# One decoder layer on one core: the second residual's rows kept on chip, and two regions moved into the expert weights' ring

## The chip, the cores and the metric

The kernel runs on one core of one Trainium2 chip. The metric is device time in microseconds (us) of one execution. Three runs of the kernel before gave 961.46, 961.75 and 962.04 us, median 961.75.

## What is computed

One decoder layer on 512 tokens of width 1024, all in float32. Token mixing (dilated attention, a convolution module, an mLSTM) is computed first; its branches are gated, merged, projected and added to x. The second part, in which the change lies, is, cut to what matters:

```
x2  = x + merged @ w_out                     # the second residual, (512, 1024)
h   = rmsnorm(x2, g_ffn)
# hierarchical MoE: top-1 of 4 groups, then top-2 of its 8 experts; 32 experts in all
hb  = silu(xb @ w_gate[e]) * (xb @ w_up[e])  # (1024, 256) each
y   = (hb @ w_down[e]) * weight              # (256, 1024)
x3  = x2 + y of the token's two experts
x4  = x3 + sigmoid(rmsnorm(x3, g_ple) @ w_pg) * (p @ w_pp)
out = rmsnorm(x4, g_final)
```

All 32 experts are run whatever the routing: each on one block of up to 64 of its tokens, and a few further blocks only if an expert has more tokens.

## The kernel before, in words

Engines run programs of their own and meet at semaphores. SyncE (SP in the profile) issues all loads and stores except the indirect ones, in an order written out by hand; a wait in its program holds back everything behind it. GpSimd (POOL) issues the indirect transfers: for each expert one gather of token rows (`normed` to `mT`, line 2210) and one scatter of result rows (`mT` to `expert_rows`, line 2216).

**Weights.** An expert's weights are an "up" piece (gate and up, 2 MiB, `up_weights`, line 551, or in halves, line 556) and a "down" piece (1 MiB, `down_weights`, line 559). They go round a ring of `RING = 7` slots; `up_w` and `down_w` say where each slot lies. Most slots are regions of the 128 KiB (per partition) tensor `arena`, one is in `yT`, the up slot of expert 6 is `hT`. The down slots of index 5 and 6 are the two halves of `x_sb`, the tensor that holds x2. In addition `early_down` names two regions of `arena`, at 120 and at 80 KiB, that are used once, for the down pieces of experts 7 and 8 (`down_of`, with a semaphore of their own, `early_loaded`). So before the first expert runs, the up pieces of experts 0 to 6 and the down pieces of experts 0 to 8 are loaded or under way.

**Why x2 leaves the chip.** Since its place is given to weights, each 128-token row block of x2 is stored to `x2_rows` in memory (`store_x2`, lines 582 to 584; 512 KB each, four of them) beside the store of its normalised rows (`store_n2`, line 588). SP then waits for these stores and for all readers of the block before it loads down pieces 5 and 6 into `x_sb`. After the experts 26 and 27 are through, `x2_row_back` (line 623) loads block 0 and 1 back, then the weights of the last stage follow (`w_pg`, `w_pp`, `p`), and behind the second half of `w_pg` blocks 2 and 3 are loaded back and `g_final`.

**The expert loop.** For n from 7 on, SP issues the up piece of expert n+1 when `up_done` says that the up products of expert n-6 are through (line 551 behind its wait), and the down piece of expert n when `down_done` says that those of expert n-7 are. For n = 7 and 8 there is no down piece in the loop. TensorE runs up(n) when both pieces of expert n have landed, then turns the next gathered block (line 1439), then runs down(n-1). All matrix products go through the helper at line 1076, the small transpose between up and down is line 1457. ScalarE applies the sigmoid (line 975), copies (line 980) and scales the result rows (line 987); VectorE multiplies (lines 2075, 2082, 2084).

**The tail.** With the last expert through, TensorE computes `p @ w_pp` (32 products of tile `hT`), ScalarE rounds `w_pg` (line 995), VectorE takes its remainder (line 2105) and copies (line 2111). When the last scatter has landed, SP loads `expert_rows` back (line 652), and VectorE adds the two result rows to x2 (lines 2134 and 2135) in its program behind six remainders. TensorE turns the sum (line 1356) and multiplies it by `w_pg`.

Of the kernel before, what the change touches and what calls it, by code (L numbers as in the profile page):

```python
# [28 lines left out]
F32 = mybir.dt.float32  # L29
# [6 lines left out]
P = 128  # L36
D = 1024
SEQ = 512
T = SEQ // P
# [25 lines left out]
RING = 7  # L65
# [58 lines left out]
def build(nc, x, consts, chan, g_mix, r_bias, g_final, w_cm, w_tm, w_if, w_gate, w_branch, w_out,  # L124
          w_router, w_expert, w_pg, w_pp, pT, out):
    normed = nc.dram_tensor("normed", [SEQ, D], F32, kind="Internal").ap()
    expert_rows = nc.dram_tensor("expert_rows", [2 * SEQ, D], F32, kind="Internal").ap()
    x2_rows = nc.dram_tensor("x2_rows", [SEQ, D], F32, kind="Internal").ap()
    bound_rows = nc.dram_tensor("bound_rows", [4 * SEQ], F32, kind="Internal").ap()

    with ExitStack() as ctx:
        offset_of = {}

        def sb(name, shape, dt=F32):
            offset_of[name] = -(-nc.sbuf_base // 32) * 32
            return ctx.enter_context(nc.sbuf_tensor(name, shape, dt))

        def sem(name):
            return ctx.enter_context(nc.semaphore(name))


        x_sb = sb("x_sb", [P, T, D])
# [29 lines left out]
        class Place:  # L172
# [63 lines left out]

        yflat = yT[:, :, :, :].rearrange("p b r s -> p (b r s)")
        ple_rows = [Place(at, memory).take(D) for at, memory in ((16, yflat), (20, yflat), (16, arena), (20, arena))]
        x_flat = x_sb[:, :, :].rearrange("p t d -> p (t d)")
        hT_flat = hT[:, :, :].rearrange("p k s -> p (k s)")  # L240
        up_w = [Place(16).take(4096), yflat[:, 0:4096]] + [Place(at).take(4096) for at in (48, 88, 0, 64)] + [hT_flat]
        down_w = [Place(32).take(2048), yflat[:, 4096:6144]] + [Place(at).take(2048) for at in (40, 112, 104)]\
            + [x_flat[:, 0:2 * D], x_flat[:, 2 * D:4 * D]]
        early_down = [Place(120).take(2048), Place(80).take(2048)]
        EARLY = RING + len(early_down)

        def down_of(n):

            return early_down[n - RING] if RING <= n < EARLY else down_w[n % RING]

        pg_w = [Place(0).take(4096), Place(24).take(4096)]
        pg_low = [parts_in("pg_low0", "arena", [P, 4096])[:, :], parts_in("pg_low1", "arena", [P, 4096], 24 * 256)[:, :]]
# [106 lines left out]
        gates_step = sem("gates_step")  # L359
        picked = sem("picked")  # L360
        routing_mm = sem("routing_mm")
        x2_spilled = sem("x2_spilled")
        prefix_ready = sem("prefix_ready")
        columns_read = sem("columns_read")
        bound_moved = sem("bound_moved")
# [59 lines left out]
        x2_ready = sem("x2_ready")  # L425
        x2_squared = sem("x2_squared")
        n2_ready = sem("n2_ready")
        n2_stored = sem("n2_stored")
        x2_turned = sem("x2_turned")
# [8 lines left out]
        ple_mm = sem("ple_mm")  # L438
        ple_copied = [sem("ple_first_half_copied"), sem("ple_second_half_copied")]
        we_loaded = [sem(f"we_loaded{b}") for b in range(RING)]  # L440
        early_loaded = sem("early_loaded")
        idx_copied = sem("idx_copied")
        rows_gathered = [sem(f"rows_gathered{b}") for b in range(ROWS)]
        rows_turned = sem("rows_turned")
# [7 lines left out]
        down_done = sem("down_done")  # L452
        y_scaled = sem("y_scaled")
# [4 lines left out]
        rows_loaded = [sem(f"rows_loaded{t}") for t in range(T)]  # L458
# [34 lines left out]
        def _(sp):  # L493
# [56 lines left out]
            def up_weights(n):  # L550
                sp.dma_start(up_w[n % RING], w_expert[n, :, 0:4096]).then_inc(we_loaded[n % RING], 16)  # L551

            def up_weights_in_halves(n):
                for half in range(2):
                    part = slice(half * 2048, (half + 1) * 2048)
                    sp.dma_start(up_w[n % RING][:, part], w_expert[n, :, part]).then_inc(we_loaded[n % RING], 16)

            def down_weights(n):
                sp.dma_start(down_of(n), w_expert[n, :, 4096:6144]).then_inc(early_loaded if RING <= n < EARLY else we_loaded[n % RING], 16)

            sp.wait_ge(yconv_ready, ROUNDS)
            sp.dma_start(wo, w_out).then_inc(wo_loaded, 16)
# [5 lines left out]
            for t in range(T):  # L568
                if t == T - 1:
                    sp.wait_ge(branch_done, 3 * KD - 1)  # L570
                sp.dma_start(x_sb[:, t, :], x[t * P:(t + 1) * P, :]).then_inc(x_loaded[t], 16)
            down_weights(RING)
            sp.wait_ge(merged, FREE + KD)
            for n in range(2):
                up_weights(n)
# [3 lines left out]
            up_weights(2)  # L579
            up_weights(3)  # L580

            def store_x2(t):
                sp.wait_ge(x2_ready, T + t + 1)
                sp.dma_start(x2_rows[t * P:(t + 1) * P, :], x_sb[:, t, :]).then_inc(x2_spilled, 16)

            def store_n2(t):
                sp.wait_ge(n2_ready, t + 1)
                sp.dma_start(normed[t * P:(t + 1) * P, :], n2[t % 2]).then_inc(n2_stored, 16)

            for t in range(T - 1):  # L590
                store_x2(t)
                store_n2(t)
            sp.wait_ge(x2_spilled, (T - 1) * 16)
            sp.wait_ge(x2_squared, T + 2)
            sp.wait_ge(x2_turned, T + 2)
            down_weights(5)
            sp.wait_ge(x2_mm, 2 * T)
            down_weights(3)
            store_x2(T - 1)
            down_weights(4)  # L600
            store_n2(T - 1)
            up_weights_in_halves(4)
            up_weights_in_halves(5)
            sp.wait_ge(logits_done, T)
            up_weights_in_halves(6)
            sp.wait_ge(x2_spilled, T * 16)
            sp.wait_ge(x2_turned, 2 * T)
            down_weights(6)
            sp.wait_ge(x2_squared, 2 * T)
            sp.wait_ge(n2_stored, T * 16)  # L610
            down_weights(RING + 1)
            for n in range(RING, NEXP):
                if n == RING:
                    sp.wait_ge(up_done, 1)
                    up_weights(n)
                if n + 1 < NEXP:
                    sp.wait_ge(up_done, n + 2 - RING)
                    up_weights(n + 1)
                if n >= EARLY:
                    sp.wait_ge(down_done, n + 1 - RING)  # L620
                    down_weights(n)
            def x2_row_back(t):
                sp.dma_start(x_sb[:, t, :], x2_rows[t * P:(t + 1) * P, :]).then_inc(rows_loaded[t], 16)

            sp.wait_ge(up_done, 26)
            sp.wait_ge(down_done, 27)
            for t in range(2):
                x2_row_back(t)
            sp.dma_start(pg_w[0], w_pg[0, :, :]).then_inc(pg_loaded[0], 16)
            sp.wait_ge(up_done, 28)  # L630
            sp.dma_start(pple_w, w_pp).then_inc(pw_loaded, 16)
            sp.dma_start(p_in, pT).then_inc(pw_loaded, 16)
            sp.wait_ge(down_done, 29)
            sp.dma_start(pg_w[1], w_pg[1, :, :]).then_inc(pg_loaded[1], 16)
            for t in range(2, T):
                x2_row_back(t)
            sp.dma_start(gfin_sb, g_final.partition_broadcast(P)).then_inc(params_loaded, 16)
            sp.wait_ge(routed, 1)
            n_over = sp.value_load(ctl[0:1, 0:1], min_val=0, max_val=MAX_OVER)
# [434 lines left out]
        def _(pe):  # L1074
            def mm(out, lhsT, rhs, start=True, stop=True):
                return pe.matmul(out, lhsT, rhs, start=start, stop=stop)  # L1076
# [377 lines left out]
            def turn_hidden(n, b2):  # L1454

                pe.wait_ge(h_swished, n + 1)
                pe.transpose(HT[:, 0:P], hs[b2], ident).then_inc(h_turned, 1)  # L1457

            def down(n, b2, w, y_free):

                pe.wait_ge(hx_ready, n + 1)
                y_free()
                for j in range(2):
                    for side in range(2):
                        at = j * 1024 + side * 512
                        last = mm(Y[b2][side * BLK:(side + 1) * BLK, :], hx[b2][:, j, :], w[:, at:at + 512], j == 0, j == 1)
                last.then_inc(down_done, 1)
# [3 lines left out]

            turn_block(0, 0, rows_gathered[0], 16, first=True)
            def expert_down(n):
                if n == RING:
                    pe.wait_ge(early_loaded, 32)
                down(n, n % 2, down_of(n), nothing if n < 2 else lambda: pe.wait_ge(y_scaled, n - 1))

            for n in range(NEXP):
                pe.wait_ge(we_loaded[n % RING], (n // RING + 1) * 32 + (16 if n % RING in (4, 5, 6) else 0) - (16 if n >= RING and n % RING < 2 else 0))
                up(n, n % 2, up_w[n % RING], nothing if n < 2 else lambda: pe.wait_ge(h_swished, n - 1),  # L1480
                   between=(lambda: turn_hidden(n - 1, (n - 1) % 2)) if n else None)
                if n + 1 < NEXP:
                    slot = (n + 1) % ROWS
                    turn_block(n + 1, slot, rows_gathered[slot], ((n + 1) // ROWS + 1) * 16)
                if n == 3:
                    over_table()
                if n:
                    expert_down(n - 1)
                if n == OVER_KNOWN:
                    pe.wait_ge(routed, 1)  # L1490
                    n_over = pe.value_load(ctl[0:1, 0:1], min_val=0, max_val=MAX_OVER)
# [27 lines left out]
            for t in range(T):  # L1519
# [3 lines left out]
                for half in range(2):  # L1523
                    n = 2 * t + half
# [28 lines left out]
        def _(dve):  # L1553
            steps = [0]

            def chain(ins):

                steps[0] += 1
                ins.then_inc(dve_step, 1)
                dve.wait_ge(dve_step, steps[0])  # L1560
# [569 lines left out]
                                      h_high[part].bitcast(F32), ALU.subtract).then_inc(h3_split, 1)  # L2130

            for t in range(T):
                dve.wait_ge(rows_loaded[t], 48)
                chain(dve.tensor_tensor(x_sb[:, t, :], x_sb[:, t, :], yk[t][:, 0, :], ALU.add))  # L2134
                dve.tensor_tensor(x_sb[:, t, :], x_sb[:, t, :], yk[t][:, 1, :], ALU.add).then_inc(x3_ready, 1)  # L2135
                if t == 0:
                    ple_second_half(3)
                    h3_remainder(0)
                    for k in range(6, KD):
                        pg_remainder(k)  # L2140
                if t == 1:
                    h3_remainder(1)
# [183 lines left out]
```

## Time and profile before

| | before |
|---|---|
| median of three runs | 961.75 us |
| the profiled execution, its device time | 961.88 us |
| its span, first to last instruction | 960.1 us |
| TensorE busy / VectorE / ScalarE / GpSimd | 93% / 51% / 36% / 20% |
| bytes moved by DMA | 182.44 MB |
| mean granted TensorE clock | 0.977 of full |
| chain that ended last: TensorE / DMA / VectorE | 80% / 11% / 4% |

The device time is 1.8 us above the span, and 0.13 us above the median of the runs. The profile is of one execution. A share of DMA is the mean busy share of the core's 16 DMA engines; where it stands at 1.01 to 1.03 all of them are busy all the time. Megabytes here are 10^6 bytes: a down piece of 1024 KB is 1.049 MB, an up piece 2.097 MB, a row block of 512 KB 0.524 MB.

### The profile page before, as it was taken

How to read it: one execution, taken by the hardware profiler on the slowest of the kernel's cores; microseconds unless marked ns; L12 is line 12 of the kernel's file. 1: busy time of each engine (PE TensorE's matmuls, PEld its weight loads, DVE VectorE, ACT ScalarE, POOL GpSimd, SP SyncE). 2: the span in 40 equal slices, each digit the busy share in tenths (PEclk: the TensorE clock that was granted, in tenths of full speed). 3: DMA queues.
4: the chain of work that ended last, by engine and by line, in shares of the span. 5: the costliest groups of instructions: out<-in, count | busy, mean ns of one | idle time of the engine just before them, and what ended most of it. 6: DMA issues, size and time to landing. Idle time of an engine off the chain costs nothing.

```text
span 960.1 us, 12099 instructions
## 1 busy us (share of the span) xinstructions
PE 893.9 (93%) x4762; PEld 655.0 (68%) x4762; DVE 492.7 (51%) x999; ACT 342.3 (36%) x574; POOL 194.2 (20%) x169
## 2 busy tenths in 40 slices
PE   5999999999999989999999999947999988779986
PEld 4788788778878858788888888844555534334675
DVE  6378679669767978633333444463111111112755
ACT  5534453544435366422222332111111111113464
POOL 0052263335226332000000000011323322221000
PEclk9999999999999999999999999968999999999998
DMA  7520321212030110822222038889999999998401
GB/s 271 176 92 19 132 67 44 98 61 84 1 132 23 66 34 1 355 116 99 95 81 86 36 131 350 308 330 363 385 417 420 421 420 421 421 418 357 183 23 66
DMA packets 29088, 182.44 MB, mean 190 GB/s; under 512 B 5840, under 2 KB 6352, under 8 KB 18152
## 3 DMA queue, kind: packets, MB, share of 16 engines
q1 hardware_dynamic: 23912, 173.26, 46.0%
q0 software_dynamic: 5120, 8.41, 2.4%
q8 instruction: 38, 0.62, 0.3%
q14 instruction: 18, 0.15, 0.0%
HBM read 175.33 MB, written 14.69 MB: 198 GB/s over the span
## 4 chain that ended last, share of the span: by engine, by line
PE 80%; DMA 11%; DVE 4%; ACT 2%; issue 1%; SPq 1%; DVEq 0%; POOLq 0%; ACTq 0%
PE bank L1076 76%; DMA arena<-in_w_expert 9%; PE bank L1439 1%; PE bank L1166 1%; DMA mT<-normed,table 1%; DMA x_sb<-in_x 1%; DMA expert_rows<-mT,table 1%; PE bank L1457 1%; DMA arena<-expert_rows 0%; SPq L551 0%; PE bank L1367 0%; DVE x_sb L2135 0%; PE bank L1092 0%; DVE x_sb L2134 0%; ACT arena L679 0%
## 5 line engine op out<-in xcount | busy, mean ns | idle before, releaser
L1076 PE MATMUL bank<-mT_parts,low_parts 128*128 128x512 f32 (+1 forms) x456 | 178.5, 394 | 0.0
L1076 PE MATMUL bank<-arena,cst 128*64 128x256 f32 (+2 forms) x904 | 132.7, 433 | 15.6 <-DMA arena<-in_w_expert 10.7
L1076 PE MATMUL bank<-mT_parts,x_parts 128*128 128x512 f32 (+1 forms) x328 | 132.4, 404 | 0.0
L1076 PE MATMUL bank<-hT_parts,x_parts 128*128 128x512 f32 (+1 forms) x328 | 129.1, 394 | 0.0
L2075 DVE TENSOR_TENSOR cst<-bank,chn 128x512 f32<-128x512 f32 x32 | 22.1, 692 | 184.3 <-PE bank L1439 184.3
L1620 DVE TENSOR_TENSOR low_parts<-arena,x_parts 128x1024 fp32r<-128x1024 f32 (+1 forms) x44 | 62.8, 1427 | 98.4 <-ACT x_parts L691 98.1
L1076 PEld LDWEIGHTS bank<-arena,cst 128*64 128x64 f32 (+1 forms) x904 | 63.1, 140 | 71.7 <-issue 29.0
L1076 PEld LDWEIGHTS bank<-mT_parts,low_parts 128*128 128x128 f32 (+1 forms) x456 | 85.0, 186 | 21.2
L1672 DVE SCALAR_TENSOR_TENSOR arena<-arena,chn 128x512 f32<-128x512 f32 x116 | 99.2, 912 | 0.0
L2210 POOL DMA_INDIRECT mT<-normed,table x32 | 33.0, 1031 | 282.1 <-DVE table L2023 268.5
L1076 PE MATMUL bank<-arena 128*128 128x64 f32 (+9 forms) x400 | 79.9, 332 | 1.2 <-DVE small L1769 1.2
L2195 POOL TENSOR_TENSOR arena<-arena 128x128 f32<-128x128 f32 (+3 forms) x32 | 40.3, 1260 | 176.1 <-ACT arena L787 176.1
L1076 PEld LDWEIGHTS bank<-mT_parts,x_parts 128*128 128x128 f32 (+1 forms) x328 | 61.1, 186 | 15.9 <-DVE low_parts L1620 0.9
L1076 PEld LDWEIGHTS bank<-hT_parts,x_parts 128*128 128x128 f32 (+1 forms) x328 | 61.0, 186 | 15.1 <-issue 0.7
L1076 PEld LDWEIGHTS bank<-arena 128*128 128x128 f32 (+1 forms) x400 | 56.3, 189 | 21.5 <-issue 14.3
L2216 POOL DMA_INDIRECT expert_rows<-mT,table x32 | 32.4, 1014 | 162.1 <-ACT mT L987 155.6
L787 ACT ACTIVATE arena<-arena,small 128x384 f32<-128x384 f32 (+3 forms) x32 | 32.6, 1020 | 55.5 <-DVE small L1769 55.5
L1076 PE MATMUL bank<-mT_parts,cm_high_b 128*128 128x512 f32 x128 | 51.3, 409 | 0.0
L928 ACT ACTIVATE arena<-bank 128x512 f32<-128x512 f32 x24 | 14.2, 595 | 102.2 <-PE bank L1076 102.2
L1076 PE MATMUL bank<-hT_parts,cm_high_b 128*128 128x512 f32 x128 | 49.2, 393 | 0.0
L987 ACT ACTIVATE mT<-bank,table_weight 128x512 f32<-128x512 f32 x32 | 22.0, 687 | 69.8 <-PE bank L1076 69.8
L1076 PE MATMUL bank<-x_parts,mT_parts 128*128 128x384 f32 x128 | 44.6, 349 | 0.0
(288 smaller groups left out, 1560.0 us busy)
## 6 DMA issues: line engine op xcount, KB each, us to landing
arena<-in_w_expert SPq DMA_DIRECT2D x21, 2048.0 KB
arena<-in_w_expert SPq DMA_DIRECT2D x24, 1024.0 KB, 13.7
arena<-in_w_cm SPq DMA_DIRECT2D x32, 512.0 KB, 3.6
arena<-in_w_gate SPq DMA_DIRECT2D x8, 1536.0 KB, 6.7
yT<-in_w_expert SPq DMA_DIRECT2D x5, 2048.0 KB
x_sb<-in_w_expert SPq DMA_DIRECT2D x8, 1024.0 KB
arena<-in_w_tm SPq DMA_DIRECT2D x4, 1536.0 KB, 7.7
arena<-in_w_branch SPq DMA_DIRECT2D x8, 768.0 KB, 8.2
```

The source lines that it names most:

```text
L787: act.activation(sc[:, u % 2, 0:n], sc[:, u % 2, 0:n], ACT.Exp, bias=nmx[:, u % 2:u % 2 + 1], accum_out=den[:, u:u + 1]).then_inc(exps_don ...
L928: act.activation(sgm[:, br], (PA, PB, S_16)[br][:, :], ACT.Sigmoid).then_inc(gate_read, 1)
L987: act.activation(yr[slot], Y[b2][:, :], ACT.Copy, scale=table_w(n)).then_inc(y_scaled, 1)
L1076: return pe.matmul(out, lhsT, rhs, start=start, stop=stop)
L1166: last = pe.transpose(TR[:, j * P:(j + 1) * P], psm[:, u % 2, j * P:(j + 1) * P], ident)
L1439: last = pe.transpose(TR[:, k * P:(k + 1) * P], xr[slot][:, k * P:(k + 1) * P], ident)
L1620: dve.tensor_tensor(low, weights, high.bitcast(F32), ALU.subtract).then_inc(done, 1)
L1672: dve.scalar_tensor_tensor(cacc[:, j % 2], ypad[:, j:j + SEQ], weight, cacc[:, j % 2], ALU.mult, ALU.add).then_inc(conv_step, 1)
L2075: dve.tensor_tensor(xT[b2], TR[:, :].rearrange("p (k h s) -> p k h s", k=KD // 2, h=2), chn[:, G_FFN:G_FFN + KD].rearrange("p (h k) -> p k ...
L2195: pool.tensor_tensor(dst[:, 0:n], sc[:, u % 2, 0:n], sc[:, u % 2, n:2 * n], ALU.add).then_inc(pool_step, 1)
L2210: pool.indirect_dma_start(out=xr[slot], out_offset=None, in_=normed_halves, in_offset=bass.IndirectOffsetOnAxis(ap=token_halves, axis=0), ...
L2216: pool.indirect_dma_start(out=expert_halves, out_offset=bass.IndirectOffsetOnAxis(ap=row_halves, axis=0), in_=yr[slot], in_offset=None, bo ...
```

## The change

The stores of x2 and the loads that bring it back are gone, and with them the tensor `x2_rows` and the semaphore `x2_spilled`. `x_sb` keeps x2 until the tail. The ring's down slots 5 and 6 are the regions at 120 and 80 KiB of `arena`. They are loaded at the places in SP's program at which the down pieces of experts 7 and 8 were: piece 5 behind the reload of x, piece 6 behind the last normalised store. The down pieces of experts 7 and 8 are issued in the loop, behind the waits for down(0) and down(1). The rest of SP's order stays.

```diff
         down_w = [Place(32).take(2048), yflat[:, 4096:6144]] + [Place(at).take(2048) for at in (40, 112, 104)]\
-            + [x_flat[:, 0:2 * D], x_flat[:, 2 * D:4 * D]]
-        early_down = [Place(120).take(2048), Place(80).take(2048)]
-        EARLY = RING + len(early_down)
-
-        def down_of(n):
-
-            return early_down[n - RING] if RING <= n < EARLY else down_w[n % RING]
+            + [Place(at).take(2048) for at in (120, 80)]
...
-            down_weights(RING)
+            down_weights(5)
...
-            def store_x2(t):
-                sp.wait_ge(x2_ready, T + t + 1)
-                sp.dma_start(x2_rows[t * P:(t + 1) * P, :], x_sb[:, t, :]).then_inc(x2_spilled, 16)
-
...
             for t in range(T - 1):
-                store_x2(t)
                 store_n2(t)
-            sp.wait_ge(x2_spilled, (T - 1) * 16)
-            sp.wait_ge(x2_squared, T + 2)
-            sp.wait_ge(x2_turned, T + 2)
-            down_weights(5)
             sp.wait_ge(x2_mm, 2 * T)
             down_weights(3)
-            store_x2(T - 1)
             down_weights(4)
             store_n2(T - 1)
...
             up_weights_in_halves(6)
-            sp.wait_ge(x2_spilled, T * 16)
-            sp.wait_ge(x2_turned, 2 * T)
-            down_weights(6)
             sp.wait_ge(x2_squared, 2 * T)
             sp.wait_ge(n2_stored, T * 16)
-            down_weights(RING + 1)
+            down_weights(6)
             for n in range(RING, NEXP):
...
-                if n >= EARLY:
-                    sp.wait_ge(down_done, n + 1 - RING)
-                    down_weights(n)
-            def x2_row_back(t):
-                sp.dma_start(x_sb[:, t, :], x2_rows[t * P:(t + 1) * P, :]).then_inc(rows_loaded[t], 16)
-
+                sp.wait_ge(down_done, n + 1 - RING)
+                down_weights(n)
             sp.wait_ge(up_done, 26)
             sp.wait_ge(down_done, 27)
-            for t in range(2):
-                x2_row_back(t)
             sp.dma_start(pg_w[0], w_pg[0, :, :]).then_inc(pg_loaded[0], 16)
...
             sp.dma_start(pg_w[1], w_pg[1, :, :]).then_inc(pg_loaded[1], 16)
-            for t in range(2, T):
-                x2_row_back(t)
...
             for t in range(T):
-                dve.wait_ge(rows_loaded[t], 48)
+                dve.wait_ge(rows_loaded[t], 32)
```

## Rows read from the trace of the kernel before

**Rows 1.** The page, whole run in 40 slices of 24 us: DMA share in tenths, GB/s.
```profile
DMA  7520321212030110822222038889999999998401
GB/s 271 176 92 19 132 67 44 98 61 84 1 132 23 66 34 1 355 116 99 95 81 86 36 131 350 308 330 363 385 417 420 421 420 421 421 418 357 183 23 66
```

**Rows 2.** Busy time by stretch: from:to, length, each engine, PEclk, DMA share, GB/s.
```profile
603.00:620.00 17.00, 17.00 (x93) 14.25 (x91) 8.73 (x28) 4.25 (x10) 0.00 (x0) 1.00 0.77 294
632.00:650.00 18.00, 6.08 (x74) 5.81 (x74) 10.40 (x39) 1.06 (x3) 4.25 (x4) 0.50 1.02 423
...
658.00:659.00 1.00, 1.00 (x10) 0.54 (x7) 0.00 (x0) 0.07 (x1) 0.00 (x0) 1.00 0.50 193
671.00:681.00 10.00, 10.00 (x96) 5.41 (x96) 2.67 (x9) 1.81 (x5) 2.04 (x2) 1.00 0.96 327
696.00:776.00 80.00, 79.21 (x562) 40.27 (x558) 15.35 (x39) 15.87 (x38) 25.46 (x25) 1.00 1.01 419
776.00:868.00 92.00, 74.15 (x501) 35.91 (x503) 12.98 (x33) 13.66 (x33) 21.67 (x22) 0.98 1.01 420
```

**Rows 3.** TensorE in order of time, stage of the experts: start, us, what, [idle before].
```profile
653.28 5.57 PE L1076 MATMUL bank<-arena,cst 128*64 128x256 f32 x32 [0.88 <-DVE cst L2075]
...
664.32 0.66 PE L1439 MATMUL bank<-cst,mT 128*128 128x128 f32 x4
...
670.64 0.66 PE L1439 MATMUL bank<-cst,mT 128*128 128x128 f32 x4
...
776.05 1.95 PE L1076 MATMUL bank<-arena,cst 128*64 128x256 f32 x16 [0.84 <-DMA x_sb<-in_w_expert]
...
867.31 1.95 PE L1076 MATMUL bank<-arena,cst 128*64 128x256 f32 x16 [1.05 <-DMA arena<-in_w_expert]
```

**Rows 4.** SyncE's issues in order of time.
```profile
570.58 0.43 SPq L559 DMA_DIRECT2D arena<-in_w_expert  x1
...
618.49 0.34 SPq L559 DMA_DIRECT2D x_sb<-in_w_expert  x1
626.94 0.33 SPq L559 DMA_DIRECT2D arena<-in_w_expert  x1
627.66 0.33 SPq L584 DMA_DIRECT2D x_rows<-x_sb  x1
...
638.75 0.33 SPq L559 DMA_DIRECT2D arena<-in_w_expert  x1
658.88 0.33 SPq L551 DMA_DIRECT2D arena<-in_w_expert  x1
...
825.18 10.12 SPq L559 DMA_DIRECT2D arena<-in_w_expert  x2
849.92 0.80 SPq L623 DMA_DIRECT2D x_sb<-x_rows  x2
```

**Rows 5.** The chain that ended last, in order of time: start, us, what.
```profile
643.65 7.58 DMA mT<-normed,table
...
883.83 5.62 DMA expert_rows<-mT,table
```

**Rows 6.** DMA issues on the page: count, KB each, median us to landing.
```profile
x_sb<-x_rows SPq DMA_DIRECT2D x4, 512.0 KB, 21.8
...
hT<-in_pT SPq DMA_DIRECT2D x1, 512.0 KB, 30.1
```

**Rows 7.** The tail in order of time, VectorE and TensorE.
```profile
882.25 14.00 PE L1076 MATMUL bank<-hT 128*128 128x512 f32 x32
...
893.46 1.27 DVE L2105 SCALAR_TENSOR_TENSOR pg_low<-arena,chn,pg_high 128x1024 fp32r<-128x1024 f32 x1
894.85 1.23 DVE L2134 TENSOR_TENSOR x_sb<-x_sb,arena 128x1024 f32<-128x1024 f32 x1
...
899.34 3.66 PE L1076 MATMUL bank<-pg_high,mT_parts 128*128 128x512 f32 x8 [0.80 <-ACT mT_parts L1034]
902.80 2.08 PE L1076 MATMUL bank<-pg_high,hT_parts 128*128 128x512 f32 x8
```

More of the change, by code:

```diff
@@ L127, in build @@
     expert_rows = nc.dram_tensor("expert_rows", [2 * SEQ, D], F32, kind="Internal").ap()
-    x2_rows = nc.dram_tensor("x2_rows", [SEQ, D], F32, kind="Internal").ap()
     bound_rows = nc.dram_tensor("bound_rows", [4 * SEQ], F32, kind="Internal").ap()
@@ L238, in build @@
         ple_rows = [Place(at, memory).take(D) for at, memory in ((16, yflat), (20, yflat), (16, arena), (20, arena))]
-        x_flat = x_sb[:, :, :].rearrange("p t d -> p (t d)")
         hT_flat = hT[:, :, :].rearrange("p k s -> p (k s)")
@@ L361, in build @@
         routing_mm = sem("routing_mm")
-        x2_spilled = sem("x2_spilled")
         prefix_ready = sem("prefix_ready")
@@ L440, in build @@
         we_loaded = [sem(f"we_loaded{b}") for b in range(RING)]
-        early_loaded = sem("early_loaded")
         idx_copied = sem("idx_copied")
@@ L558, in down_weights @@
             def down_weights(n):
-                sp.dma_start(down_of(n), w_expert[n, :, 4096:6144]).then_inc(early_loaded if RING <= n < EARLY else we_loaded[n % RING], 16)
+                sp.dma_start(down_w[n % RING], w_expert[n, :, 4096:6144]).then_inc(we_loaded[n % RING], 16)
             sp.wait_ge(yconv_ready, ROUNDS)
@@ L1473, in expert_down @@
             def expert_down(n):
-                if n == RING:
-                    pe.wait_ge(early_loaded, 32)
-                down(n, n % 2, down_of(n), nothing if n < 2 else lambda: pe.wait_ge(y_scaled, n - 1))
+                down(n, n % 2, down_w[n % RING], nothing if n < 2 else lambda: pe.wait_ge(y_scaled, n - 1))
             for n in range(NEXP):
-                pe.wait_ge(we_loaded[n % RING], (n // RING + 1) * 32 + (16 if n % RING in (4, 5, 6) else 0) - (16 if n >= RING and n % RING < 2 else 0))
+                pe.wait_ge(we_loaded[n % RING], (n // RING + 1) * 32 + (16 if n % RING in (4, 5, 6) else 0))
                 up(n, n % 2, up_w[n % RING], nothing if n < 2 else lambda: pe.wait_ge(h_swished, n - 1),
```

## The prediction, made before the changed kernel was run

> **What bounds the kernel now.** I first read the page's slices [rows 1]. From the 28th slice (about 650 us) to the 36th the DMA share stands at 8 or 9 tenths and the rate climbs to 417 to 421 GB/s: a long stretch in which the DMA engines have no time left. TensorE stands at 9 or so in the same slices, so the page alone doesn't say which of the two sets the pace. The table of stretches does [rows 2]: from 696 to 776 us TensorE is busy for 79.2 of 80 us and DMA at a share of 1.01; from 776 to 868 us DMA is still at 1.01, at 420 GB/s, but TensorE for 74.2 of 92 us only. TensorE in order of time shows the same from its side [rows 3]. While weights are in stock, an expert takes 670.64 - 664.32 = 6.32 us. Expert 19 at 776.05 is the first that waits for its weights, expert 30 at 867.31 the last. Between those two lie 11 experts in 91.26 us, so 8.30 us each, with a wait for a down or up piece before nearly every one. So the stock that was loaded ahead shrinks by 8.30 - 6.32 = 1.98 us for each expert, is gone at expert 19, and from there the end of the expert stage is the landing of bytes. What counts is then how many bytes have to land **after** the ring opens (the first refill, issued at 658.88 [rows 4]) and how long the engines stand idle after that. Before that moment time on the DMA engines is partly free: from 603 to 620 us their share is 0.77 [rows 2], and behind the last expert the stage is bound by other engines (below).
>
> **The change part by part.**
>
> *Stores of blocks 0 to 2 and down piece 5's old place.* These 3 x 0.524 MB and the 1.049 MB issued at 618.49 [rows 4] leave the stretch 603 to 627. TensorE is busy for 17.00 of 17 us there [rows 2], so nothing waits for these bytes, and I cost it at nothing. The cover is the matrix products of the output projection; without it the gain would be at most 2.62 MB / 0.420 MB per us = 6.2 us. The waits of SP that go with them held back only loads for later experts.
>
> *Store of block 3 and one down piece, from 627 on.* From 632 to 650 us the engines are full (1.02 at 423 GB/s [rows 2]) with the loads that fill the ring, issued from 626.94 to 638.75 [rows 4]. They run empty around 658.5 (share 0.50 from 658 to 659 [rows 2]), just when the first refill is issued at 658.88 [rows 4]. So before, almost no time is lost there. After, 0.524 MB (block 3) and 1.049 MB (pieces 6 and 8 become piece 6 alone) are missing: 1.573 / 0.423 = 3.7 us. The engines run empty at about 654.8 and idle until the refill, since the slots that could be refilled open only when up(0) is through. This saving goes into idle time: nothing.
>
> *Down pieces 7 and 8 in the loop.* Their 2 x 1.049 MB were moved before 658.9 (one at 570.58, one at 638.75 [rows 4]); now they are issued behind down(0) and down(1), which stand right behind the block turns at 664.32 and 670.64 [rows 3]: at about 667 and 673 us. From there to expert 30 everything is bytes, and 2.097 / 0.420 = 5.0 us are put ahead of its weights. Given back is what idle time there was behind the first refill: from 671 to 681 us the share is 0.96 against 1.01 when full [rows 2], so 0.05 x 10 = 0.5 us on the mean of the engines. The landing goes by the slowest engine, and that one may have idled less; I take 0.3, between 0 and 0.5. **Sum: +4.7 us** on the wait that ends at 867.31, between 4.5 and 5.0.
>
> The Trainium skill, "DMA: Bandwidth & Descriptors", section "Where 436 GB/s comes from", says that for transfers between HBM and SBUF the HBM side binds at about 358 GB/s. By that figure the two pieces would cost 5.9 us and the forecast would be 967.2 us. The trace doesn't agree: it holds 420 GB/s over 92 us [rows 2].
>
> *The two new waits of SP.* Behind the wait for down(0) stands the load of up 9, whose own wait (up(2)) ended as the turn at 670.64 began [rows 3], later than down(0) is through; likewise for down(1) and up 10. So nobody is held back: 0. Expert 7 starts around 697 (653.28 + 7 x 6.32 [rows 3]) and piece 7, issued at 667, waits behind at most two up pieces (10 us); covered by 20 us. If it weren't, the wait would only fall earlier, since the bytes bind later anyway.
>
> *Reload of x2, blocks 0 and 1 (issued at 849.92).* They stand in SP's queue behind the last down pieces (issued by 835.3 [rows 4]), so they don't delay the weights of expert 30. They do stand before `w_pg`, `w_pp` and `p`: 1.049 / 0.420 = 2.5 us earlier for all of these, measured from the last expert. `p` is the nearest to being late: issued three short issues behind 849.92, at about 851.7, it lands 30.1 us later [rows 6], at 881.8, and TensorE begins its products at 882.25 [rows 7]. It is on time before, by 0.4 us, and still on time after. 0.
>
> *Reload of blocks 2 and 3.* With the first two, 2.097 MB (5.0 us) leave the queue behind the last expert. The last scatter takes 5.62 us [rows 5] while such rows still load (21.8 us to landing [rows 6], so to about 889). It should land 1 to 3 us sooner. But VectorE's sum of x2 and the expert rows at 894.85 stands in its program behind the remainder that begins at 893.46 and takes 1.27, so ends at 894.73 [rows 7], and that one hangs on the products of 882.25 (14.00 us for 32, one PSUM copy after another). The gain is 894.85 - 894.73 = 0.1 us. Without that cover it would be up to 3.
>
> *The semaphore's lower value, the tensor that is gone, fewer issues on SP:* 0.
>
> **Sum against the profiled execution:** 961.88 + 4.7 - 0.1 = 966.5 us. That execution is 0.13 us above the median of the runs, so I predict **966.3 us**, 0.47% slower: the removed 4.2 MB lay where the DMA engines had room or in the tail's cover, and 2.1 MB are moved from there to where they have none.
>
> **Rivals.**
>
> *The reload does delay the last weights.* Against it stands that it is issued 15 us later than they are [rows 4]. For it: it lands only 21.8 us after its issue [rows 6], at about 871 to 872, close to the end of the last wait at 867.31; if the engines mix both, blocks 0 and 1 take 2.5 us from the experts' weights and their removal gives that back: 963.8 us. The Trainium skill, in the same page, section "Queues, rings and completion order", says that each engine consumes its descriptors in ring order but that a later one may finish its write before an earlier one; the first half speaks for my sum, the second for this rival, and this trace doesn't tell them apart.
>
> *Not slower: the first gather lands earlier, so the ring opens earlier.* TensorE waits for the first gather, 7.58 us from 643.65 on [rows 5], while the queue of weights fills the engines. If the shorter queue lets it land sooner, up(0) and all refills start sooner, and idle time of 3.7 us is used after all. The nearest row is the last scatter, of the same size in emptier engines, with 5.62 us [rows 5], so 2 us; for a bound I take 4 us, to all but the whole loss: 962.3 us. It decides from the point at which the engines run empty before the gather is done (651.2). By my count they do at 654.8, so against it.
>
> *Not slower: the tail is bound by its loads.* If `w_pg`, `p` or the expert rows, not VectorE's order, set the end, the 5.0 us that leave the tail count in full: 966.3 - 5.0 = 961.3 us. For it speaks only the margin of 0.4 us for `p`; against it the order at 893.46 to 894.85 [rows 7]. Together with the earlier gather: 957.3 us, faster.
>
> *More loss through the clock.* TensorE will wait for weights from expert 16 or 17 on (4.7 / 1.98 = 2.4 experts earlier). In 776 to 868 us the mean granted clock was 0.98 [rows 2], so short stretches at 1.2 GHz in place of 2.4 follow such waits. They hide in 1.98 us of slack for each expert, unless one falls on expert 30, 31 or the tail. One does already: the 8 products at 899.34 took 3.66 us against 2.08 for the next 8 [rows 7]. One more costs 1.6 us, this one's absence gives 1.6: 964.7 to 967.9 us. That belongs to my forecast's own range. Two more: 969.5 us.
>
> **How the numbers follow.** My sum, with one such stretch more or less, 0.70; the reload among the last weights (963.8) 0.10; the earlier gather (962.3) 0.08; the tail bound by loads (961.3) 0.05; both of the last (957.3) 0.04; more loss (969.5) 0.03. About 0.2% (1.9 us) is what a measurement of this kernel can tell from no change, so "the same" is 959.8 to 963.7. Slower: 0.70 + 0.03 + half of 0.10 = 0.78. The same: 0.05 + 0.08 + 0.05 = 0.18. Faster: 0.04. The range 963.0 to 968.3 holds my forecast's own 964.5 to 968.1 (the bounds of the clock and of 4.5 to 5.0) and the first rival; left out are 0.17 below and 0.03 above.
>
> **What would show it.** After: the DMA share drops to near 0 from about 655 to 659.5; TensorE's first wait for weights comes at expert 16 or 17, near 757 to 763 us; the last one ends at 871.5 to 872.3; from there to the end the tail is as long as before (92.8 us from 867.31 to 960.1) within 0.2 us, but for the clock. The last scatter lands in less than 5.6 us without moving the end. Wrong it would be if the engines stay full between 650 and 659, if the last wait ends at about 869.5 (reload among weights), or if the tail shrinks by more than 1 us.

## The result, and the profile after

The changed kernel took 964.31 us (median of 11 runs, 962.93 to 966.20), the kernel before beside it 962.61 us (11 runs, 961.46 to 964.51). The ratio is 1.0019, 95% interval 1.0011 to 1.0027: slower by 1.7 us (1.1 to 2.6), where +4.6 us was forecast. The sign and the range held; the forecast loss was 2.7 times the measured one. A second set of 11 runs of the changed kernel gave 964.03 us, ratio 1.0018 (1.0009 to 1.0027).

The profiled execution took 964.68 us with a span of 962.9 us, 2.8 us above that of before (960.1). The medians differ by less. Single executions of one kernel spread over 3 us, so below I first compare stages inside the executions.

Stretches of after (from:to, length, busy time of each engine, PEclk, DMA share, GB/s), to be held against [rows 2]:

```profile
603.00:620.00 17.00, 17.00 (x89) 14.17 (x88) 9.23 (x28) 4.34 (x10) 0.00 (x0) 1.00 0.50 207
...
655.00:661.00 6.00, 6.00 (x36) 3.75 (x34) 0.00 (x0) 0.32 (x1) 0.66 (x1) 0.65 0.10 27
...
671.00:681.00 10.00, 10.00 (x99) 5.67 (x97) 2.67 (x9) 1.52 (x4) 3.30 (x4) 1.00 1.00 419
...
776.00:868.00 92.00, 75.28 (x503) 36.07 (x499) 12.99 (x33) 13.67 (x33) 21.52 (x21) 0.96 1.01 421
```

Three things are to be seen. The stores are gone from 603 to 620 (207 GB/s against 294), and TensorE is still busy for all of it. From 655 to 661 the DMA engines are all but idle (share 0.10, 27 GB/s), as forecast. And from 671 to 681 they move 419 GB/s, where before they moved 327.

The gather, the first refill and the last wait for weights of after, against [rows 3 to 5] (timelines of TensorE and SyncE):

```profile
652.77 1.11 PE L1408 MATMUL bank<-cst,mT 128*128 128x128 f32 x4 [7.90 <-DMA mT<-normed,table]
...
660.63 0.33 SPq L541 DMA_DIRECT2D arena<-in_w_expert  x1
...
772.67 1.95 PE L1045 MATMUL bank<-arena,cst 128*64 128x256 f32 x16 [2.03 <-DMA arena<-in_w_expert]
...
871.85 1.95 PE L1045 MATMUL bank<-arena,cst 128*64 128x256 f32 x16 [1.05 <-DMA arena<-in_w_expert]
```

From the first refill to the last wait it is 871.85 - 660.63 = 211.2 us, where before it was 867.31 - 658.88 = 208.4 [rows 3, 4]. This distance is the measure of the weights' stream, free of what happened ahead of it, and it grew by 2.8 us, not by 4.7. The refill itself came 1.75 us later than before. Of that, 1.1 us was there before the first removed store (the issue behind the branch stage stands at 597.24 against 596.15). It is no work of the change: in a second execution of the changed kernel this issue stands at 596.32.

The tail of after, against [rows 5, 7]:

```profile
891.10 0.10 POOL L2217 MEMSET small<- 128x1 f32 x1 [1.75 <-DMA expert_rows<-mT,table]
...
898.00 1.27 DVE L2072 SCALAR_TENSOR_TENSOR pg_low<-arena,chn,pg_high 128x1024 fp32r<-128x1024 f32 x1
899.19 1.22 DVE L2101 TENSOR_TENSOR x_sb<-x_sb,arena 128x1024 f32<-128x1024 f32 x1
...
903.68 2.13 PE L1045 MATMUL bank<-pg_high,mT_parts 128*128 128x512 f32 x8 [0.80 <-ACT mT_parts L1003]
```

GpSimd waits 1.75 us for the last scatter, against 4.96 before. It gains nothing: VectorE's sum begins right behind its remainder, and the first product with `w_pg` comes 903.68 - 871.85 = 31.8 us behind the last wait, against 32.0 before. But its 8 products take 2.13 us and not 3.66: no stretch at 1.2 GHz falls on them. So the tail, from the last wait to the end, is 962.9 - 871.85 = 91.1 us, against 92.8.

### The profile page after: what moved, and what is told of

It is laid out like the page before. It is cut to its first block, busy times and chain, and to the rows that moved or that the text cites. A ratio compares the mean times of both kernels' runs of the same rounds, so it can differ in the third digit from the quotient of the medians.

```text
span 962.9 us, 12089 instructions
## 1 busy us (share of the span) xinstructions
PE 893.5 (93%) x4762; PEld 653.5 (68%) x4762; DVE 492.8 (51%) x999; ACT 342.5 (36%) x574; POOL 194.0 (20%) x169
## 4 chain that ended last, share of the span: by engine, by line
PE 78%; DMA 15%; DVE 4%; ACT 2%; issue 1%; SPq 0%; DVEq 0%; ACTq 0%; POOLq 0%
PE bank L1045 74%; DMA arena<-in_w_expert 12%; PE bank L1408 1%; PE bank L1135 1%; DMA arena<-in_w_branch 1%; DMA mT<-normed,table 1%; DMA x_sb<-in_x 1%; PE bank L1426 0%; PE bank L1336 0%; DVE x_sb L2102 0%; PE bank L1061 0%; ACT arena L648 0%; DVE x_sb L2101 0%; SPq L541 0%; DVE hT_parts L2096 0%
## 5 line engine op out<-in xcount | busy, mean ns | idle before, releaser
L1045 PE MATMUL bank<-arena,cst 128*64 128x256 f32 (+2 forms) x960 | 147.9, 447 | 16.3 <-DMA arena<-in_w_expert 13.7
L1045 PEld LDWEIGHTS bank<-arena,cst 128*64 128x64 f32 (+1 forms) x960 | 67.0, 141 | 78.7 <-issue 34.6
```

## The experiments

**The traffic alone.** The kernel before without stores and reload, its ring untouched (VectorE then waits for two loads of rows in place of three; the kernel leaves x2 out of its result).

```diff
-                store_x2(t)
...
-            sp.wait_ge(x2_spilled, (T - 1) * 16)
...
-            store_x2(T - 1)
...
-            sp.wait_ge(x2_spilled, T * 16)
...
-            for t in range(2):
-                x2_row_back(t)
...
-            for t in range(2, T):
-                x2_row_back(t)
...
-                dve.wait_ge(rows_loaded[t], 48)
+                dve.wait_ge(rows_loaded[t], 32)
```

> The kernel before without the four stores of x2 and the four loads that bring it back; the ring stays as it was. Left out: x2 is lost, so the sums of the tail are taken with weights in its place. Theory A (these 4.2 MB lie in free time of the DMA engines or behind the tail's VectorE chain): 0.0 to -0.3 us against before, and the last wait of TensorE for weights ends as long after the first refill as before (208.4 us). Theory B (the reload takes time from the last experts' weights): -2.5 us, and that distance shrinks to about 206.

Measured: 962.38 us (11 runs), ratio to before 1.0002 (0.9991 to 1.0013). The last wait ends 869.96 - 661.14 = 208.8 us behind the first refill:

```profile
869.96 1.95 PE L1068 MATMUL bank<-arena,cst 128*64 128x256 f32 x16 [1.07 <-DMA arena<-in_w_expert]
```

Theory A holds: 4.2 MB of traffic are worth nothing here, within 1.3 us. Theory B is out: the distance did not shrink.

**The traffic put back into the changed kernel** (the same lines, added to the changed SyncE program, with one wait for the stores ahead of the reload).

> The changed kernel with the stores and the reload put back at their old places; the ring is the changed one. Theory A: 0.0 to +0.3 us against the changed kernel, so about +1.8 to +2.8 us against before; the distance from first refill to last wait stays that of the changed kernel (211.2 us). Theory B: +2.5 us on top, so +4 to +5 against before, distance about 213.7.

Measured: 963.59 us, ratio to before 1.0014 (1.0005 to 1.0023); distance 869.87 - 659.11 = 210.8 us. The distance is that of the changed kernel, so theory A holds here too; against the changed kernel's median the time is 0.4 to 0.7 us lower, which lies within the spread, and it falls short of the +1.8 us or more that I expected. The last scatter is slow again (GpSimd waits 5.07 us for it), and the sum of VectorE starts 0.17 us late, not more:

```profile
892.44 0.10 POOL L2234 MEMSET small<- 128x1 f32 x1 [5.07 <-DMA expert_rows<-mT,table]
...
897.47 1.22 DVE L2118 TENSOR_TENSOR x_sb<-x_sb,arena 128x1024 f32<-128x1024 f32 x1 [0.17 <-DMA arena<-expert_rows]
```

So the reload does delay the scatter, and the cover that the prediction named takes all of it.

**The ring alone.** The kernel before with its stores and reload, and down pieces 7 and 8 both in the loop (the counts that TensorE waits for follow).

```diff
-        EARLY = RING + len(early_down)
+        EARLY = RING
...
-            down_weights(RING)
...
-            down_weights(RING + 1)
```

> The kernel before, in which only the down pieces 7 and 8 are moved into the loop; x2 is stored and reloaded as before. By the prediction's sum (5.0 us of bytes, 0.3 given back) +4.7 us. Theory A2 (the DMA engines were short of work from 671 to 681 us before, 327 against 419 GB/s, so one piece of 2.5 us fits in there): +2.5 to +2.8 us, with 410 GB/s or more in the stretch from 12 to 22 us after the first refill.

Measured: 964.20 us, ratio 1.0012 (1.0003 to 1.0021). Distance 871.28 - 660.59 = 210.7 us, +2.3 us on before. This one part, without any of the traffic removed, makes the whole slowdown of the change (964.31 and 964.03 us). The +4.7 us of the sum is out. Theory A2 comes close by the distance; the medians moved by 1.6 us, less than its 2.5. The last wait, and the stretch from 12 to 22 us behind the refill:

```profile
871.28 1.95 PE L1074 MATMUL bank<-arena,cst 128*64 128x256 f32 x16 [1.04 <-DMA arena<-in_w_expert]
...
672.59:682.59 10.00, 10.00 (x97) 5.40 (x97) 2.67 (x9) 1.81 (x5) 2.05 (x2) 1.00 1.00 414
```

The like stretch of before, also from 12 to 22 us behind its refill:

```profile
670.88:680.88 10.00, 10.00 (x95) 5.43 (x95) 2.67 (x9) 1.81 (x5) 2.04 (x2) 1.00 0.94 321
```

**Half of it:** only piece 8 in the loop (`EARLY = RING + 1`).

> The kernel before, in which only down piece 8 is moved into the loop; piece 7 stays early. By the prediction's sum half the loss, +2.2 to +2.5 us. Theory A2: the one piece fills the room from 671 to 681 us and costs -0.2 to +0.4 us.

Measured: 963.63 us, ratio 1.0008 (0.9998 to 1.0019). Distance 871.01 - 660.95 = 210.1 us, +1.6. The medians can't tell this run from either side; the distance lies between the two expectations. The row says why the room isn't filled at once:

```profile
672.95:682.95 10.00, 10.00 (x97) 5.41 (x97) 2.67 (x9) 1.81 (x5) 2.05 (x2) 1.00 0.96 365
```

365 GB/s against 321 in the like stretch of before: piece 8 is issued at about 675, too late for the first part of the gap, and uses (365 - 321) x 10 = 0.44 MB of it, 1.0 us. 2.5 - 1.0 = 1.5 us remain, as measured. Both expectations missed; that of about 0 had assumed that the room is there whenever the piece comes.

**Spending the idle stretch.** If the DMA engines idle from 655 to 661 us anyway, the loads that fill them while TensorE waits for the first gather can be held back. One line in the changed kernel, ahead of the up piece of expert 6:

```diff
             sp.wait_ge(logits_done, T)
+            sp.wait_ge(rows_gathered[0], 16)
             up_weights_in_halves(6)
```

> The changed kernel; SyncE issues the up and down piece of expert 6 only when the first gather has landed. If the idle stretch of the DMA engines before the first refill (about 5 us at 655 to 660.6 us) is where the removed bytes went, it can be spent earlier: the first gather, 8.2 us beside full engines, lands in 3 to 4 us, the ring opens 4 to 5 us sooner, the engines are idle around the gather in place of the 655 to 660 stretch, and the time falls by 4 to 5 us against the changed kernel: 959 to 960.5 us. If the gather's time is its own and not contention, the ring opens at the same time and the time stays within 1 us of the changed kernel's.

Measured: 961.10 us, ratio to before 0.9983 (0.9972 to 0.9993), 2.9 us below the changed kernel beside it (964.03). The wait for the gather and the last wait:

```profile
648.45 1.12 PE L1409 MATMUL bank<-cst,mT 128*128 128x128 f32 x4 [3.72 <-DMA mT<-normed,table]
...
867.85 1.95 PE L1046 MATMUL bank<-arena,cst 128*64 128x256 f32 x16 [1.06 <-DMA arena<-in_w_expert]
```

The wait for the gather falls from 7.90 to 3.72 us, the refill is issued at 657.03 (after: 660.63), and the last wait ends 4.0 us sooner than in after, at an unchanged distance (210.8 us). So about half of the gather's time came from the full queue beside it, and the idle time was real. The gain is less than the 4 to 5 us expected, in part because TensorE runs the up products of expert 0 earlier and at a lower clock: they take 6.55 us, against 5.84.

The same line in the kernel before:

> The kernel before with the same wait (held back: up piece 6 and down pieces 6 and 8). Bytes decide: at the landing of the gather 4.2 MB are still to come before the refills, so the engines have no idle stretch left, and the ones of before (1.3 us at 659, 2.2 us worth between 671 and 681) are used: -3 to -4 us against before, about 959 us, so no better than 1 us away from the changed kernel with the hold. If instead idle time before the ring opens is lost in the kernel before, it gets 1 to 3 us slower.

Measured: 959.80 us (9 runs), ratio 0.9972 (0.9962 to 0.9982), 2.8 us faster than before (3 to 4 expected) and 1.3 us below the run with the hold in the changed kernel, a difference that barely stands out of the spread. The wait for the gather is 4.58 us (before 7.29); the last wait ends at 865.78, 1.5 us sooner than before. Two stretches of it:

```profile
657.00:661.00 4.00, 3.12 (x28) 2.06 (x24) 1.93 (x8) 1.56 (x2) 0.00 (x0) 0.98 1.00 420
671.00:681.00 10.00, 10.00 (x99) 5.48 (x95) 2.06 (x9) 1.93 (x4) 2.05 (x2) 1.00 1.00 389
```

Both gaps of before are nearly filled (there 193 GB/s from 658 to 659 and 327 from 671 to 681 [rows 2]). This is the fastest kernel of the study by its median, and it keeps the two early pieces and the spill.

**Opening the ring sooner.** The changed kernel, with the up piece of expert 7 in two halves, the first issued when the up products of expert 0 are half through (`up_half_done`, a new semaphore that TensorE raises there).

```diff
-                    sp.wait_ge(up_done, 1)
-                    up_weights(n)
+                    for half in range(2):
+                        part = slice(half * 2048, (half + 1) * 2048)
+                        sp.wait_ge((up_half_done, up_done)[half], 1)
+                        sp.dma_start(up_w[0][:, part], w_expert[n, :, part]).then_inc(we_loaded[0], 16)
```

> The changed kernel; the up piece of expert 7 is loaded in halves, the first as soon as expert 0 has used the first half of its own. The ring opens about 2.8 us sooner (half of the 5.8 us of up(0)) without any change to the gather: -2 to -2.8 us against the changed kernel, 961.5 to 962.3 us, if idle time of the DMA engines before the first refill passes one to one to the last wait. If it doesn't, 964.3 us.

Measured: 964.09 us, the same as the changed kernel (964.03). A miss. The first half is issued at 657.48, but the distance to the last wait grows to 870.23 - 657.48 = 212.8 us:

```profile
658.00:660.00 2.00, 1.76 (x16) 0.95 (x12) 0.20 (x1) 0.75 (x1) 0.00 (x0) 1.00 0.77 197
...
664.00:666.00 2.00, 2.00 (x16) 0.95 (x14) 0.66 (x2) 0.28 (x1) 0.00 (x0) 1.00 0.75 188
666.00:668.00 2.00, 2.00 (x16) 1.00 (x14) 1.88 (x6) 0.69 (x1) 0.00 (x0) 1.00 0.67 279
```

The engines run dry again at 664 to 667 us: up 8 is issued at 664.76, when up(1) is through, and what was won in the first gap is lost in a second. So opening the ring sooner for one piece alone gave nothing here: the load behind it still waits for up(1). With the hold up(0), up(1) and all the refills came sooner.

**Repeats for the spread.** The changed kernel (11 runs) and twice the kernel before (one execution each), unchanged.

> The changed kernel once more, for the spread of its stages: median 964 to 965 us; distance from the first refill to the last wait 210.7 to 211.4 us; the tail 91.1 us where the clock stays at 2.4 GHz and 92.6 us where the products behind the first turn of x3 meet a stretch at 1.2 GHz.

> The kernel before once more, for its profile alone: distance from the first refill to the last wait 208.4 to 208.8 us. If the time between that distance's growth (+2.1 to +2.8 us) and the growth of the median (+1.7 us) lies in the tail, the products behind the first turn of x3 meet a stretch at 1.2 GHz here again and the tail is 92.5 to 92.8 us; if that stretch falls by chance, it is 91.1 us.

> As the run before: distance 208.4 to 208.8 us, tail 92.5 to 92.8 us or 91.1 us.

The changed kernel again: median 964.03 us, refill at 660.09, expert 30 at about 871.2 (31.8 us ahead of its first product with `w_pg`, at 903.02), distance 211.1. The kernel before: 867.69 - 658.87 = 208.8 and 868.48 - 660.17 = 208.3. With the traffic runs there are four executions with pieces 7 and 8 early (208.3 to 208.8 us) and four with both in the loop (210.7 to 211.2 us). The two groups stand 1.9 us apart at least and 2.3 us on their means, so the growth is no chance; the +2.8 of the first pair lies at its upper end. The tails of the kernel before are 92.0 and 91.2 us: in the first, 8 products later in the tail take 3.28 us in place of 2.13; in the second none do.

```profile
926.17 3.28 PE L1076 MATMUL bank<-pg_high,mT_parts 128*128 128x512 f32 x8 [1.90 <-ACT mT_parts L1034]
```

So the tail of the kernel before ranged over 1.6 us in three executions, by whether and where a slow stretch of the clock fell on it. The kernel without the traffic had such a stretch too (tail 92.5 us):

```profile
901.79 3.34 PE L1068 MATMUL bank<-pg_high,mT_parts 128*128 128x512 f32 x8 [0.80 <-ACT mT_parts L1026]
```

## Why the prediction was right in sign and too large

*What bounds the kernel:* right, but not from the refill on. The ring alone moved the time, and the DMA engines move about 420 GB/s up to the last wait in all these kernels, from about 32 us behind the refill at the latest. In the first 12 us behind it they moved only 350 GB/s in before, and less than 420 in the next 20. The slices of rows 1 had shown it: 363 and 385 GB/s from 648 to 696 us, beside a DMA share of 9 tenths.

*Stores and piece 5's old place at nothing:* right. Without all the traffic the kernel before took the same time (1.0002), and with both pieces in the loop the distance was the same with piece 5 in its old place (210.7 us) and in its new one (210.8). *Block 3 and one down piece go into idle time:* right; the engines run dry at about 655 (forecast 654.8, in an execution that was 1.1 us late by then) and idle until the refill.

*Pieces 7 and 8 in the loop, +4.7 us:* here the sum failed, in the term "given back". The 5.0 us of bytes are right. But I took the idle time behind the refill from the DMA **share**, 0.96 against 1.01 over 10 us, so 0.5 us at most, and put it at 0.3. The same row had the rate beside it, 327 GB/s [rows 2], and that is what bytes go by: (420 - 327) x 10 = 0.93 MB, 2.2 us. In the trace the 16 KB packets of that stretch took 0.74 us each on average, against 0.61 in the like stretch of after. The median was 0.61 in both; the mean is raised by 30 of the 165 packets, of 0.8 to 2.5 us, and 19 of these begin 1 to 3 us behind the issues of up pieces at 670.75 and 677.07. As I read it, the busy share hid the shortage: packets that came when the engines had little left to do took longer, and all of that time counts as busy. No run isolates this; that there was room in the stretch is shown by the 414 to 419 GB/s it carries once the pieces are issued there. After, the stretch runs at 419 GB/s, so 0.92 MB more go through, 2.2 us. 5.0 - 2.2 = 2.8 us, which is what the distance grew by in this pair. Over the four executions of each ring the rates from 12 to 22 us behind the refill are 321 to 330 and 412 to 418 GB/s, and from 22 to 32 us 407 to 417 and 426 to 428: 0.9 and 0.14 MB, 2.5 us together. That leaves 2.5 us, where 2.3 were measured. The cause of the gap, by the times of the issues, is the order of the refills: one up piece for each of the first experts (2.1 MB in 6.3 us, 333 GB/s asked of engines that move 420), because the down pieces 7 and 8 were already in. The changed ring asks for them just there. The experiment with one piece shows the same term half used.

*The two new waits, the tail's 0.1 us, the margin of `p`:* right; the part of the tail up to the first product with `w_pg` is 31.8 us against 32.0, and VectorE's order hid 3.2 us of the scatter.

*From 2.3 or 2.8 to the measured 1.7 us* (1.1 to 2.6 by the interval): open in part. The profiled executions of after and before differ by 2.1 to 3.2 us in span, so the three profiles of before may lie on its fast side (961.5 to 961.9 us, median of its runs 962.6). The clock in the tail would fit the rest. In the five profiled executions with pieces 7 and 8 early (before three times, no traffic, before with the hold) the tails are 91.2 to 92.8 us, mean 92.0, and a stretch at 1.2 GHz falls on three of them. In the seven with one or both in the loop they are 91.0 to 91.2 us, and none has one. Twelve executions don't show that the ring's order decides it.

*Signs named beforehand:* the first wait for weights was to come at expert 16 or 17; it came at expert 18 (772.67), against 19 before, since the loss of stock was smaller. The last wait was to end at 871.5 to 872.3: it ended at 871.85, but 1.1 us of that was a late start, which made a smaller loss look like mine: that sign came true by luck. The tail was to be wrong if it shrank by more than 1 us; it shrank by 1.7, of which 1.5 is the stretch at 1.2 GHz on the 8 products (3.66 against 2.13 us) that was excepted.

*Luck in the range:* the measured 964.31 us lies below the 964.5 to 968.1 that the sum itself allowed. It is inside the stated range only because that was drawn wide enough for the reload's 963.8 us, whose mechanism the experiments rule out.

*Rivals:* the reload among the last weights (963.8 us) would have come closest to the measured time, but both traffic experiments rule its mechanism out. The first gather did not land earlier by itself (7.90 us against 7.29): the queue was still full beside it. As a mechanism it was real, though: made to happen by the hold, it gave 2.9 us. The tail bound by loads is ruled out by the same experiments as the reload.

The 358 GB/s of the Trainium skill ("DMA: Bandwidth & Descriptors", section "Where 436 GB/s comes from") for the HBM side, weighed in the prediction, found no support: the changed kernel holds 421 GB/s from 776 to 868 us.

## What to carry to other kernels

Traffic removed from this kernel was worth nothing where the DMA engines did not set the end. So ask first in which stretch each byte moves, and whether bytes that were loaded ahead are moved behind the point where the ring opens (its first refill). Read a DMA stretch by its GB/s against the rate of a full stretch, not by its busy share, and look for gaps right behind the opening of a ring, where each step asks for less than the engines can move. A small transfer that the whole kernel waits for should not be issued into a full queue of loads that nobody needs yet: holding those back by one wait gave 2.8 us in the kernel before and 2.9 us in the changed one.

## What the runs showed of the hardware

A DMA share of 0.96 went with 327 GB/s and one of 1.00 with 419 GB/s in the like stretch (671 to 681 us), with 16 KB packets that took 0.74 and 0.61 us on average. An indirect transfer of 64 rows of 4 KB made TensorE wait 7.1 to 8.0 us in seven kernels in which it was issued beside a full queue (DMA share 1.01, 414 GB/s from 646 to 652 us in the changed kernel), and 3.7 and 4.6 us in the two where loads were held back (0.68, 207 GB/s in the changed kernel with the hold). GpSimd's wait for the last scatter went from 4.96 to 1.75 us when the reload was gone beside it, and was 5.07 us again with the reload put back. Short stretches at 1.2 GHz fell on the tail in some executions of one and the same kernel and not in others: the same 8 products took 3.66 or 2.13 us, with a wait of 0.80 us before them in both.
